# A transformer-like block pair on one core: the start of each head's triangular solve is re-ordered on VectorE, ScalarE and TensorE

## What is computed

```python
def gated_delta_rule_chunked(q, k, v, g, beta):
    ...
    G = jnp.cumsum(g, axis=-1)
    decay = jnp.exp(jnp.where(tril, G[..., :, None] - G[..., None, :], -jnp.inf))
    k_beta = k * beta[..., None]
    L = jnp.where(strict, jnp.einsum('bnhid,bnhjd->bnhij', k_beta, k) * decay, 0.0)
    sol = lax.linalg.triangular_solve(eye + L, rhs, left_side=True, lower=True)
    ...
k = l2norm(k)        # k * rsqrt(sum(k*k) + EPS)
o = o * lax.rsqrt(jnp.mean(o * o, axis=-1, keepdims=True) + EPS) * norm_g
```

## Time and profile before

| | |
|---|---|
| median of 3 runs | 1433.12 us (1433.01 to 1435.26) |
| the profiled execution, its own time | 1433.34 us |
| its span | 1431.6 us |
| PE busy | 1357.2 us (95%) |
| DVE busy | 796.2 us (56%) |
| ACT busy | 582.8 us (41%) |
| POOL busy | 243.4 us (17%) |
| mean granted TensorE clock | 0.982 |

### The profile page before, as it was taken

One profiled execution on the slowest core, in us unless ns is written; L12 is line 12 of the kernel. 1 busy time (PEld: TensorE's weight loads), 2 busy tenths in 40 slices (PEclk: granted clock), 3 DMA queues, 4 the chain that ended last, 5 costly groups with the idle time before them and its releaser, 6 DMA issues.

```text
span 1431.6 us, 20293 instructions
## 1 busy us (share of the span) xinstructions
PE 1357.2 (95%) x6903; PEld 1073.5 (75%) x6903; DVE 796.2 (56%) x1634; ACT 582.8 (41%) x965; POOL 243.4 (17%) x509
## 2 busy tenths in 40 slices
PE   6998989898898989999989999999997999999998
PEld 4777868686786868888768888888885767677776
DVE  4757465564646554344366564356645698943532
ACT  5434444353444432222234342243443455445522
POOL 1113030221303020000340000000032533232200
PEclk9999999999999999999999999999999999999999
DMA  4222222222222223333323323333233312222111
GB/s 151 74 75 59 74 59 73 59 73 73 59 73 59 73 60 88 88 103 103 89 59 103 91 82 99 110 103 88 70 99 81 91 45 60 60 60 71 62 45 74
DMA packets 208502, 111.46 MB, mean 78 GB/s; under 512 B 6826, under 2 KB 206793, under 8 KB 208457
## 3 DMA queue, kind: packets, MB, share of 16 engines
q1 hardware_dynamic: 208073, 110.86, 27.2%
q0 software_dynamic: 384, 0.03, 0.0%
HBM read 108.75 MB, written 2.10 MB: 77 GB/s over the span
## 4 chain that ended last, share of the span: by engine, by line
PE 82%; DVE 11%; issue 3%; POOL 2%; ACT 2%; DMA 0%; POOLq 0%; DVEq 0%; ACTq 0%
PE gb L596 67%; PE gd L954 2%; PE gb L1005 2%; PE gd L1005 2%; PE gd L933 1%; DVE selb L1810 1%; DVE small L1809 1%; POOL elt L1966 1%; POOL Ue L1969 1%; DVE act_a L1409 1%; PE gd L944 1%; DVE selb L1799 1%; PE gd L608 1%; PE gd L656 1%; PE gd L766 0%
## 5 line engine op out<-in xcount | busy, mean ns | idle before, releaser
L596 PE MATMUL gb<-act_a,whi 128*128 128x512 f32 x2800 | 970.8, 408 | 8.9 <-ACT act_a L1028 4.5
L596 PEld LDWEIGHTS gb<-act_a,whi 128*128 128x128 f32 x2800 | 531.1, 190 | 132.2 <-issue 10.5
L596 PE MATMUL gb<-act_a,wlo 128*128 128x512 f32 x1488 | 585.8, 394 | 0.0
L596 PEld LDWEIGHTS gb<-act_a,wlo 128*128 128x128 f32 x1488 | 283.8, 191 | 57.3 <-issue 4.1
L1374 DVE TENSOR_TENSOR wlo<-raw,whi 128x1024 fp32r<-128x1024 f32 x190 | 234.3, 1233 | 135.2 <-ACT whi L1020 134.6
L1020 ACT ACTIVATE whi<-raw 128x1024 fp32r<-128x1024 f32 x212 | 223.0, 1052 | 172.4 <-PE gb L596 141.9
L596 PE MATMUL gb<-act_b,whi 128*128 128x512 f32 x304 | 109.2, 389 | 0.0
L2058 POOL TENSOR_TENSOR wlo<-raw,whi 128x1024 fp32r<-128x1024 f32 x22 | 52.7, 2396 | 145.9 <-ACT whi L1020 145.9
L596 PEld LDWEIGHTS gb<-act_b,whi 128*128 128x128 f32 x304 | 57.1, 188 | 11.9
L2024 POOL TENSOR_TENSOR zs<-zs,ca 128x512 f32<-128x512 f32 x3 | 5.4, 1786 | 321.7 <-ACT ca L1023 321.7
L1979 POOL TENSOR_TENSOR rr<-ss,rr 128x4 f32<-128x4 f32 x8 | 1.6, 199 | 306.3 <-DVE ss L1575 306.3
(11 more groups left out here) (420 smaller groups left out, 1578.2 us busy)
## 6 DMA issues: line engine op xcount, KB each, us to landing
raw<-in_w_in_dram SPq DMA_DIRECT2D x103, 512.0 KB, 3.6
raw<-in_w_up_dram SPq DMA_DIRECT2D x44, 512.0 KB, 3.7
raw<-in_w_down_dram SPq DMA_DIRECT2D x16, 384.0 KB, 3.1
raw<-in_w_down_dram SPq DMA_DIRECT2D x16, 320.0 KB, 3.0
raw<-in_w_a_out_dram SPq DMA_DIRECT2D x8, 512.0 KB, 3.5
raw<-in_w_b_out_dram SPq DMA_DIRECT2D x8, 512.0 KB, 3.5
raw<-in_w_o_dram SPq DMA_DIRECT2D x8, 512.0 KB, 3.5
raw<-in_w_out_dram SPq DMA_DIRECT2D x8, 512.0 KB, 3.4
```

The costliest lines, as they stand in the source:

```text
L596: ins = pe.matmul(gb[:, b, :], l, r, start=(first and m == 0), stop=(last and m == len(todo) - 1))
```

## The change

DVE now takes a head's decay and key sums before anything else of (3,0) to (3,2): the last two steps of the head before (31 and 32) move behind `dec` and behind `Lp`, and unit 4's `wlo` moves from (3,1) to (3,2), behind `Lp`, `Le`, `Ue` and three shuffles. The factor 1/(sum+EPS) is a `reciprocal` on DVE in place of a power and a square on POOL; POOL keeps the square root for the value's length, off that path. ACT loads the exponential's table by a small activation `warm` after (2,3), ahead of unit 4's `whi`, and copies v's first tap (L1113) two quarters later. The shuffles start two quarters earlier. All levels (steps 10 to 16) become steps 11 to 17, one quarter later on PE, DVE and ACT. In the first head PE spreads the decay sums one quarter later. Line numbers after L190 grow by 1 to 12 in the changed kernel.

The core of the diff:

```diff
@@ PE step
-                elif g == 11:
+                elif g == 12:
                     pe.wait_ge(t_ready, 3 * h + 1)
...
@@ PE head
-                        if s == 2 and m == 3:
+                        if (s, m) == ((3, 0) if peeled else (2, 3)):
                             step(-1, h)
@@ ACT head
                     for m in range(4):
+                        if s == 3 and m == 3:
+                            first_half(h, 2)
                         if m == 1:
-                            if s > 0:
+                            if s > 0 and s != 3:
                                 first_half(h, s - 1)
...
+                        if m == 3 and s == 2:
+                            sc.activation(warm[:], mhalf[:], ACT.Exp)
@@ DVE shuffles
-                if 4 <= g <= 8:
-                    for m in range((g - 4) * 3, (g - 3) * 3):
+                if 2 <= g <= 6:
+                    for m in range((g - 2) * 3, (g - 1) * 3):
@@ DVE step
                 elif g == 1:
                     dve.wait_ge(sq_ready, 2 * h + 1)
-                    dve.tensor_reduce(ss[:, 0, :], Ti[:], AX_X, ALU.add).then_inc(ss_ready, 1)
-                elif g == 2:
+                    link(dve.tensor_reduce(ss[:, 0, :], Ti[:], AX_X, ALU.add))
+                    link(dve.tensor_scalar(rr[:, 0, :], ss[:, 0, :], EPS, None, ALU.add))
+                    link(dve.reciprocal(rr[:, 1, :], rr[:, 0, :]))
+                    dve.tensor_tensor(rr[:, R_B2, :], hc[:, C_BETA:C_BETA + TC], rr[:, 1, :], ALU.mult).then_inc(b2_ready, 1)
                     dve.wait_ge(kk_done, 2 * h + 1)
                     dve.wait_ge(dec_ready, h + 1)
                     dve.tensor_tensor(LT[:], bank(gd[:, 1, :]), dec[:], ALU.mult).then_inc(lt_ready, 1)
-                elif g == 3:
+                elif g == 2:
+                    dve.wait_ge(b2_ready, h + 1)
                     dve.wait_ge(lt_ready, 2 * h + 1)
-                    dve.wait_ge(b2_ready, h + 1)
...
-                elif g == 10:
+                elif g == 11:
                     dve.wait_ge(el_done, (E - 1) * h + (E - 1))
@@ DVE head
-                        if s >= 3:
-                            shuffles((s - 3) * 4 + m, h)
-                        if late and m == 1:
+                        if s >= 4:
+                            shuffles((s - 3) * 4 + m)
+                        if late and m == 1 and s != 3:
                             split(N_B + 8 * h + s + 1, N_B + s + 1)
...
-                        elif not peeled:
+                        elif not peeled and (s, m) != (2, 3):
                             step(20 + s * 4 + m, h - 1)
...
-                        if s == 3 and m == 2 and not peeled:
+                        if s == 3 and m == 0 and not peeled:
+                            step(31, h - 1)
+                        if s == 3 and m >= 2:
+                            shuffles(m)
+                        if s == 3 and m == 2:
+                            split(N_B + 8 * h + s + 1, N_B + s + 1)
+                        if s == 3 and m == 3 and not peeled:
                             step(32, h - 1)
@@ POOL head_a
-                pool.wait_ge(ss_ready, 2 * h + 1)
-                link(pool.tensor_tensor(rr[:, 0, :], ss[:, 0, :], eps_one[:], ALU.add))
-                link(pool.tensor_tensor(rr[:, 1, :], rr[:, 0, :], mhalf[:], ALU.pow))
-                link(pool.tensor_tensor(rr[:, 2, :], rr[:, 1, :], rr[:, 1, :], ALU.mult))
-                pool.wait_ge(hc_ready, h + 1)
-                pool.tensor_tensor(rr[:, R_B2, :], hc[:, C_BETA:C_BETA + TC], rr[:, 2, :], ALU.mult).then_inc(b2_ready, 1)
+                pool.wait_ge(b2_ready, h + 1)
+                pool.tensor_tensor(rr[:, R_BKD, :], hc[:, C_BKD:C_BKD + TC], rr[:, 1, :], ALU.mult)
+                link(pool.tensor_tensor(rr[:, 2, :], rr[:, 0, :], mhalf[:], ALU.pow))
```

More of the change, by code:

```diff
@@ L78 @@
 E = 16
-R_B2, R_KLEN, R_BKD = 3, 0, 7
+R_B2, R_KLEN, R_BKD = 3, 2, 7
 MASKED = -3.0e38
@@ L144, in schedule @@
     return at
-TO_2K = 80
+TO_2K = 72
 class Steps:
@@ L193, in hybrid_block_kernel @@
         ide = sb("ide", [P, E])
+        warm = sb("warm", [P, TC])
         hm = sb("hm", [P, 2])
@@ L697, in step @@
                     ins.then_inc(y_done, 1)
-                elif g == 12:
+                elif g == 13:
                     pe.wait_ge(zeros_ready, 1)
@@ L705, in step @@
                     ins.then_inc(z_done, 1)
-                elif g == 13:
+                elif g == 14:
                     pe.wait_ge(zeros_ready, 1)
@@ L714, in step @@
                     ins.then_inc(y_done, 1)
-                elif g == 14:
+                elif g == 15:
                     pe.wait_ge(zeros_ready, 1)
@@ L722, in step @@
                     ins.then_inc(z_done, 1)
-                elif g == 15:
+                elif g == 16:
                     pe.wait_ge(zeros_ready, 1)
@@ L731, in step @@
                     ins.then_inc(y_done, 1)
-                elif g == 16:
+                elif g == 17:
                     pe.wait_ge(zeros_ready, 1)
@@ L1147, in head @@
                     for m in range(4):
+                        if s == 3 and m == 3:
+                            first_half(h, 2)
                         if m == 1:
-                            if s > 0:
+                            if s > 0 and s != 3:
                                 first_half(h, s - 1)
-                            elif not peeled:
+                            elif s == 0 and not peeled:
                                 first_half(h - 1, 7)
@@ L1477, in decay_columns, with shuffles @@
                 link(dve.tensor_copy(cols(C_EL), hct(sm[:, 9, 0:32])))
-            def shuffles(g, h):
-                if 4 <= g <= 8:
-                    for m in range((g - 4) * 3, (g - 3) * 3):
+            def shuffles(g):
+                if 2 <= g <= 6:
+                    for m in range((g - 2) * 3, (g - 1) * 3):
                         dve.stream_shuffle(row_at(m), Le[:, :, m + 1:E], [i // E * E + m for i in range(B)]).then_inc(sh_ready, 1)
@@ L1659, in _ @@
             with dve.Fori(1, HEADS) as h:
-                own.enter(h - 1, 12)
+                own.enter(h - 1, 15)
                 head(h, False)
@@ L1953, in head_a @@
             def head_a(h):
-                pool.wait_ge(ss_ready, 2 * h + 1)
-                link(pool.tensor_tensor(rr[:, 0, :], ss[:, 0, :], eps_one[:], ALU.add))
-                link(pool.tensor_tensor(rr[:, 1, :], rr[:, 0, :], mhalf[:], ALU.pow))
-                link(pool.tensor_tensor(rr[:, 2, :], rr[:, 1, :], rr[:, 1, :], ALU.mult))
-                pool.wait_ge(hc_ready, h + 1)
-                pool.tensor_tensor(rr[:, R_B2, :], hc[:, C_BETA:C_BETA + TC], rr[:, 2, :], ALU.mult).then_inc(b2_ready, 1)
-                pool.tensor_tensor(rr[:, R_BKD, :], hc[:, C_BKD:C_BKD + TC], rr[:, 2, :], ALU.mult)
-                pool.tensor_tensor(rr[:, R_KLEN, :], rr[:, 0, :], rr[:, 1, :], ALU.mult).then_inc(klen_ready, 1)
+                pool.wait_ge(b2_ready, h + 1)
+                pool.tensor_tensor(rr[:, R_BKD, :], hc[:, C_BKD:C_BKD + TC], rr[:, 1, :], ALU.mult)
+                link(pool.tensor_tensor(rr[:, 2, :], rr[:, 0, :], mhalf[:], ALU.pow))
+                pool.tensor_tensor(rr[:, R_KLEN, :], rr[:, 0, :], rr[:, 2, :], ALU.mult).then_inc(klen_ready, 1)
                 pool.wait_ge(klen_ready, h + 1)
@@ L1971, in head_a @@
                     pool.wait_ge(el_done, (E - 1) * h + m + 1)
-                pool.wait_ge(ss_ready, 2 * h + 2)
+                pool.wait_ge(ss_ready, h + 1)
                 link(pool.tensor_tensor(rr[:, 6, :], ss[:, 1, :], eps_one[:], ALU.add))
@@ L1978, in head_b @@
                 pool.wait_ge(q_ready, h + 1)
-                link(pool.tensor_tensor(rr[:, 2, :], ss[:, 2, :], rr[:, 6, :], ALU.add))
-                pool.tensor_tensor(rr[:, 5, :], rr[:, 2, :], mhalf[:], ALU.pow).then_inc(or_ready, 1)
+                link(pool.tensor_tensor(rr[:, 5, :], ss[:, 2, :], rr[:, 6, :], ALU.add))
+                pool.tensor_tensor(rr[:, 5, :], rr[:, 5, :], mhalf[:], ALU.pow).then_inc(or_ready, 1)
             head_a(0)
             with pool.Fori(1, HEADS) as h:
-                own.enter(h - 1, 5)
+                own.enter(h - 1, 3)
                 head_b(h - 1)
```

## The result

| | before | after |
|---|---|---|
| median | 1433.83 us (4 runs, 1433.01 to 1435.26) | 1410.95 us (4 runs, 1409.15 to 1411.73) |
| ratio, with its 95% interval | | 0.9838 (0.9821 to 0.9855) |
| span of the profiled execution | 1431.6 us | 1408.5 us |
| mean granted TensorE clock | 0.982 | 0.987 |

The change makes the kernel 1.6% faster, 23 us, against the forecast 1411 us.

The account below looks back on a forecast made before the run. PE, 95% busy, was taken to bound the kernel by its work plus losses. A loop head's loss falls from 5.37 to 2.2, times 7 is 22.3, less 1.2 for the first head is 21: 1412, with small terms 1411 us; range 1401 to 1424.

Parts of the forecast that it names:

- The path that it named: L695 waits through `Up` and POOL's elimination for the first shuffle; `Lp` started only at 186.49, three us after `LT`.
- The three remaining waits: PE's waits per loop head after the change: unit 4's `wlo` 1.2, L695 0.4, L729 0.6, 2.2 us together.
- 5.37: PE's loss per loop head before the change, in us: 3.72 at L695, 1.40 for half clock, 0.25 at L736.
- 1.40 for the slow clock: Behind L695's wait, 2.8 us of PE work at clock 0.50 costs 1.4 us in each loop head.
- up to 1.4 more: First head: unit 4's 3.1 us wait might lower the clock and add this many us to the 1.2 forecast.
- POOL is done 2 us before: POOL ends the elimination near 198.5, at worst 199; PE comes to L695 at about 201.0.
- rival 4: DVE's wide instructions hold POOL up 2 us more, L695 still waits 2 or more: 1420 to 1427; chance 0.05.
- cover 1.4 us of the wait: At L695, levels a quarter later put six more matmuls, 1.4 us of PE work, ahead of the wait.
- It lies below the 2.32 us that keeps the clock: Unit 4's new wait of 1.2 us, bounds 0.8 to 1.7, costs only itself, since a 2.32 wait kept full clock.
- Rival 3: Unit 4's wait grows to about 3.7 and the clock falls behind it, deciding from 3.0 on: 1441 us; chance 0.05.
- Rival 1: ACT's table load holds ACT longer than its row, by 1.28; unit 4 waits 2.5 at full clock: 1420; chance 0.06.
- the rule beside it: The Trainium skill's drain of about 1.38 per table switch on ACT: unit 4 waits 2.6, sum some 9 us worse.

Follow-up runs that it names:

- e1: The changed kernel with its levels (steps 11 to 17) a quarter earlier again, so the earlier start alone: 1412.40 us.
- e3: The changed kernel without the small early exponential, so the table load stands between K's square and the exponential again: 1415.02 us.
- e7: The changed kernel with the factor formed on POOL again (power, square, product) in place of DVE's reciprocal: 1417.55 us.
- e2: The changed kernel with unit 4's `wlo` back at its old place, ahead of K's sum: 1408.06 us.
- e4: The changed kernel with the convolution's rounding moved from (6,3) to (7,0) and (7,1), behind the step that feeds L730: 1404.88 us.
- e10: The changed kernel with unit 4's `wlo` ahead of K's sum, the convolution's rounding behind the last level and the filter behind `Y`: 1392.75 us.
- e6: The changed kernel with `Up` and `Tp` ahead of the filter's two instructions on DVE: 1410.83 us.
- e5: The kernel before with only the level steps 10 to 16 made 11 to 17 on PE, DVE and ACT: 1433.21 us.
- e8: The kernel before with the levels a quarter later and the filter's two instructions behind `Up` and `Tp` on DVE: 1425.98 us.

## Why the prediction was right, and where it was not

**The path that it named is the one that decides.** e1 shows it: the earlier start alone makes 25.6 of the 26.3 us gained in the seven heads. Of its parts, the early table is worth 4.6 there (e3) and the reciprocal on DVE 4.9 (e7), and the later `wlo` of unit 4 costs 2.9 (e2). What the moves of steps 31 and 32 and the earlier shuffles bring, each by itself, no run shows. The start went as its steps said, in a third head that ran 1 us ahead of the forecast: sum, factor, `LT`, `Lp`, `wlo` were put at 181.05 to 185.4 and came at 180.08 to 184.42, the reciprocal at 0.18 as chosen.

**The three remaining waits.** Unit 4: 1.2 forecast, 1.0 measured. L696 (then L695): 0.4 and 0.4. L730 (then L729): 0.6 and 0.6. L736's 0.25 went. e2 and e4 take the first and the third away and show what stands behind each.

**The size.** 22.3 was forecast for the seven heads (3.2 each), 26.3 came. With the measured waits, 5.37 - 2.03 = 3.3 is due for a head that took 62.2 us, and 3.4 came in each of five. The 5.37 itself holds there: e10, with none of these waits and no slow clock, has 56.8, which is 5.4 less than 62.2. The other two took 63.4 (the last head was shorter, before and after), and there the term "1.40 for the slow clock" was too small: I had read one head and multiplied it by seven. The head after it has the same wait and a longer stretch at half clock. Before, 3.4 us behind its wait, which ends at 264.61, and in the third head at the same distance:

```profile
268.00:270.00 2.00, 2.00 (x36) 1.68 (x36) 0.53 (x2) 0.61 (x2) 0.00 (x0) 0.50 0.61 161
```

```profile
206.00:208.00 2.00, 2.00 (x50) 1.46 (x48) 0.53 (x2) 0.92 (x3) 0.00 (x0) 1.00 0.74 195
```

Two heads of 1.2 us more give 2.4; the measured 0.2 less at unit 4 gives 1.4 more. The first head was put at 1.2 more and cost 1.1, though not by the same terms: it has 0.26 at L730 in place of 0.6, and 3.07 at unit 4 with the clock kept up. With the clock down, as in e1, e3, e4 and e6, this head is 1.3 to 1.7 longer, which is the "up to 1.4 more" that the prediction left open; that it stayed up in the profiled execution was luck. The time was met more closely than the loop, since 2.0 us elsewhere, no part of the change as far as the trace shows, went the other way. That the forecast 1411 is the median itself is luck to that extent.

**The step that failed: POOL's spare.** "POOL is done 2 us before", with its end put near 198.5, was wrong. I allowed 0.8 for one wide DVE instruction more; in fact the shuffles' earlier start puts the elimination beside three `wlo`, the last step of the head before and the filter, and it takes 15.2 us, 2.4 more. That used up the spare: POOL ended 0.07 after the filter. The wait still came out at 0.4, since DVE's chain, which I had summed, ended then as well: the tie hid the error. The first half of rival 4 (POOL held up by 2 us more) did happen, and it cost nothing only by that tie.

**What the later levels bring.** I had them cover 1.4 us of the wait in every head. e5 says that they bring nothing in time alone, and e1 that they bring 0.1 us a head beside the earlier start: what they cover at L696, they give back to the filter, which has come ahead of `Up`, and at L730, where the rounding now stands ahead of the feed. The prediction had both of these in its sum, but as small prices of a large step; e4 shows that the second alone was worth 4.5 us over the seven heads, where the whole step brought 0.6.

**The clock.** "It lies below the 2.32 us that keeps the clock" was right for a wait of 1.0, and no wait of up to 1.8 at these places lowered it in any run. As a bound it was no good beyond that length: e8 lost the clock seven times behind 2.4 us. Rival 3 would thus have begun earlier than the 3.0 that I gave it.

**The load.** Rival 1 and the rule beside it did not come: the load cost its row, and leaving it out (e3) made the kernel 4 us slower.

## What to carry to other kernels

When an engine waits for a chain, look first at when the chain starts and what is queued ahead of its first link; delaying the waiting engine brings little if its feeder's queue is filled with other work at the same time. Put wide VectorE instructions that read two operands from SBUF where GpSimd is not on the path, and count each one that falls beside a GpSimd chain as up to its own length. Of a loss that recurs, read every occurrence before multiplying one.
